# The gated output of a state space layer: four fp32 panels against three fp32r passes with an operand split, and the layer norm behind it cut by column halves

## The reference

```
y = y.transpose(2, 0, 1, 3, 4).reshape(Bsz, S, G * H) + f32(d_skip) * f32(u)
g = jax.nn.gelu(y).astype(u.dtype)
val, gate = jnp.split(g @ w_glu + b_glu, 2, axis=-1)     # w_glu: 1024 x 2048
y = val * jax.nn.sigmoid(gate)
...
x = layer_norm_2(ALPHA * x + (1.0 + g_m) * y, ln_mix_g, ln_mix_b)
u = x * (1.0 + sc_f) + sh_f
y = moe_ffn(u, w_router, w13, w2)          # top 2 of 8 experts, router on u
x = layer_norm_2(ALPHA * x + (1.0 + g_f) * y, ln_ffn_g, ln_ffn_b)
```

## Time and profile before

| | us |
|---|---|
| runs (3) | 2682.57, 2685.78, 2686.11; median 2685.78 |
| profiled execution, its own time | 2683.08 |
| span of its trace | 2681.2 |
| PE busy | 2482.5 (93%) |
| DVE busy | 1778.1 (66%) |
| ACT busy | 1248.6 (47%) |
| first gated product starts | 1731.62 |
| last gated sum done | 1799.11 |
| router sums done | 1824.49 |
| first expert product starts | 1842.56 |

### The profile page before, as it was taken

How to read it: one execution, slowest core, us unless ns; L and a number is a source line. 1 busy time by engine, 2 the same in 40 slices (tenths; PEclk the granted TensorE clock), 3 DMA queues, 4 the chain that set the end, 5 groups by cost and what they waited for, 6 DMA issues and landing times.

```text
span 2681.2 us, 31991 instructions
## 1 busy us (share of the span) xinstructions
PE 2482.5 (93%) x12549; PEld 1974.6 (74%) x12549; DVE 1778.1 (66%) x1920; ACT 1248.6 (47%) x1290; POOL 157.7 (6%) x142
## 2 busy tenths in 40 slices
PE   7999999999999999899799964587999999999996
PEld 6878768878788688799548852236887888888885
DVE  5863457767733488671535559517888888888887
ACT  4432434344323343442224445305676676677674
POOL 0000000000000000000100006400000000000000
PEclk9999999999999999998899986597999999999998
DMA  8757367667671676540235530124998998998994
GB/s 312 270 200 184 84 180 276 247 230 247 247 177 54 207 271 223 178 145 32 94 118 190 195 119 31 63 94 146 347 347 325 349 345 324 348 345 326 346 349 181
DMA packets 303444, 586.15 MB, mean 219 GB/s; under 512 B 61454, under 2 KB 96996, under 8 KB 303212
## 3 DMA queue, kind: packets, MB, share of 16 engines
q1 hardware_dynamic: 285952, 521.07, 56.1%
q0 software_dynamic: 16960, 63.47, 7.2%
q10 hardware_dynamic: 428, 0.15, 0.0%
HBM read 583.59 MB, written 1.06 MB: 218 GB/s over the span
## 4 chain that ended last, share of the span: by engine, by line
PE 85%; DVE 9%; ACT 3%; issue 2%; DMA 0%; POOL 0%; DVEq 0%; SPq 0%; ACTq 0%
PE psum L851 19%; PE psum L853 18%; PE psum L852 18%; PE psum L1315 3%; PE psum L884 3%; PE psum L2518 2%; PE psum L1322 2%; PE psum L1377 2%; PE psum L2015 2%; PE psum L974 2%; DVE ring_r L1051 1%; PE psum L2632 1%; PE psum L1942 1%; PE psum L2655 1%; ACT ring_r L1045 1%
## 5 line engine op out<-in xcount | busy, mean ns | idle before, releaser
L1051 DVE TENSOR_TENSOR ring_r<-ring,ring_r 128x2048 fp32r<-128x2048 f32 x286 | 652.6, 2289 | 302.7 <-ACT ring_r L1045 302.3
L1045 ACT CAST ring_r<-ring 128x2048 fp32r<-128x2048 f32 x286 | 545.3, 1910 | 513.6 <-PE psum L853 424.0
L853 PE MATMUL psum<-ring_r,arena_r 128*128 128x512 f32 (+1 forms) x1560 | 597.3, 383 | 0.0
L851 PE MATMUL psum<-ring_r,arena_r 128*128 128x512 f32 (+1 forms) x1016 | 401.1, 395 | 9.8 <-DVE arena_r L2650 5.2
L852 PE MATMUL psum<-ring_r,arena_r 128*128 128x512 f32 (+1 forms) x1016 | 391.4, 385 | 0.0
L1051 DVE TENSOR_TENSOR ring_r<-ring,tail_r 128x2048 fp32r<-128x2048 f32 x143 | 327.3, 2289 | 96.4 <-ACT tail_r L1045 96.3
L1045 ACT CAST tail_r<-ring 128x2048 fp32r<-128x2048 f32 x143 | 273.1, 1910 | 145.5 <-PE psum L853 140.4
L853 PEld LDWEIGHTS psum<-ring_r,arena_r 128*128 128x128 f32 x1560 | 294.8, 189 | 57.7
L853 PE MATMUL psum<-ring_r,z_r 128*128 128x512 f32 (+1 forms) x840 | 311.1, 370 | 0.0
L851 PEld LDWEIGHTS psum<-ring_r,arena_r 128*128 128x128 f32 x1016 | 192.2, 189 | 57.6 <-issue 18.1
L852 PEld LDWEIGHTS psum<-ring_r,arena_r 128*128 128x128 f32 x1016 | 192.7, 190 | 37.6 <-issue 1.9
(11 more groups left out here) (410 smaller groups left out, 3337.2 us busy)
## 6 DMA issues: line engine op xcount, KB each, us to landing
ring<-in_moe_w SPq DMA_DIRECT2D x264, 1024.0 KB, 6.9
arena<-in_ada_w POOLq DMA_DIRECT2D x48, 1024.0 KB, 9.1
ring<-in_ffn_wg SPq DMA_DIRECT2D x44, 1024.0 KB, 7.3
ring<-in_ffn_wu SPq DMA_DIRECT2D x44, 1024.0 KB, 7.3
ring<-in_ffn_wd SPq DMA_DIRECT2D x44, 1024.0 KB, 6.9
ring<-in_ffn_w SPq DMA_DIRECT2D x33, 1024.0 KB, 5.3
ring<-in_mlstm_w_in SPq DMA_DIRECT2D x8, 2048.0 KB, 8.6
ring<-in_mlstm_w_out SPq DMA_DIRECT2D x4, 2048.0 KB, 7.7
```

Of the source, the lines that this page charges most:

```text
L851: pe.matmul(dst, lhs_low, rhs, start=start, stop=False)
L853: return pe.matmul(dst, lhs, rhs_low, start=False, stop=stop)
L1045: act.copy(upper[i % UPPERS], place(PN[r.key, i])).then_inc(upper_ready, 1)
L1051: dve.tensor_tensor(low, raw, upper[i % UPPERS], ALU.subtract).then_inc(lower_ready, 1)
```

## The change

The gated output is computed in three fp32r passes. The four panels come in the order gate then value, for column half 0 and then 1, each in two halves of k. The first half of panel 0 in high x high w and low x high w stands on PE ahead of `outputs(7)`, the last output sum; its low w follows it. ACT makes the upper parts (`up{i}`) and the upper parts of gelu's result (`xh0`, `xh1`); DVE makes the lower parts. The bias is loaded by SP before the weight panels, split in an upper and a lower part as well, and added in two products of one row. For column half 1 the order is gate t0, value t0, gate t1, value t1. DVE joins the product with the gate row, the residual and the statistics to each quarter (`gated_dve`), so the layer norm of stage 8 starts with the center for tile 0 as soon as that tile's last value sum is there. The router takes tile 0 before tile 1 is transposed.

```diff
-    def ln_dve(dve, step, m, source, ready, between=None, measured=None):
+    def ln_dve(dve, step, m, source, ready, between=None, measured=None, own=None):
...
         def residual(t):
+            if own is not None:
+                own(t)
+                return
...
         def statistics(t):
-            for i in range(2):
-                dve.bn_stats(bn[:, t, i, :], z[:, t, i * 512:(i + 1) * 512]).then_inc(*step.one())
+            if own is None:
+                for i in range(2):
+                    dve.bn_stats(bn[:, t, i, :], z[:, t, i * 512:(i + 1) * 512]).then_inc(*step.one())
...
-                PN["s5", "glu", i] = rg.take()
+                PN["s5", "glu", i] = rg.take(i, over=s5P.after(("gate01", "val01", "gate11", "val11")[i]))
...
+        sp.wait_ge(x_ready, NT * 8)
+        sp.dma_start(z_row[0:1, :], A["s5_b_glu_2"]).then_inc(bias_landed, 16)
         w = rows(A["s5_w_glu_2"][0])
...
-        pool.wait_ge(*s5P.after("y7"))
-        pool.dma_start(z_row[0:1, :], A["s5_b_glu_2"]).then_inc(bias_landed, 16)
...
+        act.copy(glu_ones, ones[0:1, :]).then_inc(*s5A.inc("ones"))
+        act.wait_ge(bias_landed, 16)
+        act.copy(bias_hi, z_row[0:1, :]).then_inc(*s5A.inc("bias"))
         gelu(act, 0)
+        glu_upper_act(act, 0, None)
+        glu_upper_act(act, 1, s5V.after(f"in{S5_UNITS - 1}"))
         gelu(act, 1)
-        for i in range(4):
-            act.wait_ge(*s5P.after(f"glu{i}"))
-            act.activation(sig[:, i, :], bank(2 * i + 1), ACT.Sigmoid).then_inc(*s5A.inc(f"sig{i}"))
+        glu_upper_act(act, 2, s5P.after("y7"))
+        glu_upper_act(act, 3, None)
+        gate_sig(act, 0, 0)
+        gate_sig(act, 0, 1)
+        glu_upper_act(act, 4, s5P.after("gate01"))
+        glu_upper_act(act, 5, None)
+        glu_upper_act(act, 6, s5P.after("val01"))
+        glu_upper_act(act, 7, None)
+        gate_sig(act, 1, 0)
...
+        if half == 0:
+            act.wait_ge(*s5G.after("x13"))
+        act.copy(glu_xh[:, part, :], xT[:, part, :]).then_inc(*s5A.inc(f"xh{half}"))
...
+        low_x(0)
+        glu_lower_dve(dve, 0)
         skip_u(KD - 1)
-        for i in range(4):
-            h_, t = divmod(i, 2)
-            dve.wait_ge(*s5A.after(f"sig{i}"))
-            ins = dve.tensor_tensor(y_sum[:, t, h_ * CHUNK:(h_ + 1) * CHUNK], bank(2 * i), sig[:, i, :], ALU.mult)
+        low_x(1)
+        glu_lower_dve(dve, 1)
+        dve.wait_ge(*s5A.after("bias"))
+        dve.tensor_tensor(bias_low, z_row[0:1, :], bias_hi, ALU.subtract).then_inc(*s5V.inc("bias_low"))
+        for i in range(2, 6):
+            glu_lower_dve(dve, i)
+        dve.wait_ge(lnp_landed, lnp_count(8))
+        for t in range(NT):
+            gated_dve(dve, step, 0, t)
+        for i in range(6, 8):
+            glu_lower_dve(dve, i)
+
+    def gated_dve(dve, step, h_, t):
...
+        dve.wait_ge(*s5A.after(f"sig{h_}{t}"))
+        link(dve.tensor_tensor(gate, gate, lnp[:, 2, cols], ALU.mult))
+        dve.wait_ge(*s5P.after(f"val{h_}{t}"))
+        link(dve.tensor_tensor(total, bank(4 * h_ + 2 * t), gate, ALU.mult))
+        link(dve.scalar_tensor_tensor(total, x[:, t, cols], ALPHA, total, ALU.mult, ALU.add))
+        dve.bn_stats(bn[:, t, h_, :], total).then_inc(*step.one())
...
+        for t in range(NT):
+            pe.wait_ge(*s5A.after("up0"))
+            pe.wait_ge(*s5V.after(f"scan{S5_UNITS - 2 + t}"))
+            value(0, t, 0, False, False, True)
+        pe.wait_ge(*s5V.after("xl0"))
+        for t in range(NT):
+            value(0, t, 0, True, False)
+        outputs(KD - 1)
+        pe.wait_ge(*s5V.after("low0"))
+        for t in range(NT):
+            value(0, t, 0, False, True)
+        pe.wait_ge(*s5A.after("xh1"))
+        for t in range(NT):
+            value(0, t, 1, False, False)
+        pe.wait_ge(*s5V.after("xl1"))
+        for t in range(NT):
+            value(0, t, 1, True, False)
+        pe.wait_ge(*s5V.after("low1"))
+        for t in range(NT):
+            value(0, t, 1, False, True)
+            biased(0, t)
+        for p, tiles in ((1, (0, 1)), (2, (0,)), (3, (0,)), (2, (1,)), (3, (1,))):
+            for t in tiles:
+                for half in range(2):
+                    pe.wait_ge(*s5A.after(f"up{2 * p + half}"))
+                    value(p, t, half, False, False, half == 0)
+                    value(p, t, half, True, False)
+                for half in range(2):
+                    pe.wait_ge(*s5V.after(f"low{2 * p + half}"))
+                    value(p, t, half, False, True)
+                biased(p, t)
...
-    def route_pe(pe):
+    def route_pe(pe, q):
         for t in range(NT):
+            if t > 0:
+                turn_x(pe, q, t)
+            pe.wait_ge(xT_ready, 4 * q + 2 * (t + 1))
...
                         ln_act(act, m, t)
+                        if m == 8 and t == 0:
+                            gate_sig(act, 1, 1)
...
-                    ln_dve(dve, step, m, lambda t: y_sum[:, t, :], [step.now()] * NT)
+                    ln_dve(dve, step, m, None, [s5V.after("low7")] * NT, own=lambda t: gated_dve(dve, step, 1, t))
```

More of the change, by code:

```diff
@@ L380, in s5_dve_order @@
                 names.append(f"y{k - 1}")
-        return names + [f"y{KD - 1}"]
-    s5P = Events(sem("s5_pe"), [f"bt{i}" for i in range(4)] + s5_pe_order() + [f"glu{i}" for i in range(4)])
+        return names + ["xl0", "low0", f"y{KD - 1}", "xl1", "low1", "bias_low"] + [f"low{i}" for i in range(2, 8)]
+    s5P = Events(sem("s5_pe"), [f"bt{i}" for i in range(4)] + s5_pe_order() +
+                 ["gate00", "gate01", "val00", "val01", "gate10", "val10", "gate11", "val11"])
     s5A = Events(sem("s5_act"), ["dt", "mag", "abs", "cos"] + [f"bt{i}" for i in range(4)] + ["phase0", "abs0", "rot0"] +
                  [n for k in range(KD) for n in ((f"phase{k + 1}", f"ct{k}", f"abs{k + 1}", f"rot{k + 1}") if k + 1 < KD
-                                                 else (f"ct{k}",))] + ["gelu0", "gelu1"] + [f"sig{i}" for i in range(4)])
+                                                 else (f"ct{k}",))] + ["ones", "bias", "gelu0", "xh0", "up0", "up1", "gelu1", "xh1", "up2", "up3", "sig00", "sig01"] +
+                 [f"up{i}" for i in range(4, 8)] + ["sig10", "sig11"])
     s5V = Events(sem("s5_dve"), ["lam_dt", "turn", "b_wide"] + s5_dve_order())
@@ L2397, in gelu, with glu_place, glu_high, glu_upper_act @@
         act.wait_ge(*s5V.after(f"y{k1 - 1}"))
-        part = xT[:, k1 - KD // 2:k1, :]
-        act.activation(part, part, ACT.Gelu_apprx_tanh).then_inc(*s5A.inc(f"gelu{half}"))
+        part = slice(k1 - KD // 2, k1)
+        act.activation(xT[:, part, :], xT[:, part, :], ACT.Gelu_apprx_tanh).then_inc(*s5A.inc(f"gelu{half}"))
+        act.wait_ge(*s5A.after(f"gelu{half}"))
+        if half == 0:
+            act.wait_ge(*s5G.after("x13"))
+        act.copy(glu_xh[:, part, :], xT[:, part, :]).then_inc(*s5A.inc(f"xh{half}"))
+    def glu_place(i, of):
+        pn = PN["s5", "glu", i // 2]
+        return of[:, pn.slot, (i % 2) * HALF:(i % 2 + 1) * HALF].rearrange("p (k n) -> p k n", n=CHUNK)
+    def glu_high(i):
+        return glu_hi[2 * (i // 2 % 2) + i % 2]
+    def glu_upper_act(act, i, freed):
+        if freed is not None:
+            act.wait_ge(*freed)
+        act.wait_ge(*landed(PN["s5", "glu", i // 2]))
+        act.copy(glu_high(i), glu_place(i, ring)).then_inc(*s5A.inc(f"up{i}"))
+    def glu_lower_dve(dve, i):
+        dve.wait_ge(*s5A.after(f"up{i}"))
+        dve.tensor_tensor(glu_place(i, ring_r), glu_place(i, ring), glu_high(i), ALU.subtract).then_inc(*s5V.inc(f"low{i}"))
+    def gate_sig(act, h_, t):
+        act.wait_ge(*s5P.after(f"gate{h_}{t}"))
+        act.wait_ge(*s5G.after(f"x{S5_UNITS - 1}"))
+        act.activation(sig[:, 2 * h_ + t, :], bank(4 * h_ + 2 * t + 1), ACT.Sigmoid).then_inc(*s5A.inc(f"sig{h_}{t}"))
     def s5_dve(dve, step):
@@ L2503, in s5_pe, with value @@
                     turn_c(n // 2)
-            if n % 2 == 0 and n >= 4:
+            if n % 2 == 0 and n >= 4 and n // 2 - 2 < KD - 1:
                 outputs(n // 2 - 2)
[L2507 to L2524, removed]
+        def value(p, t, half, x_low, w_low, first=False):
+            of = xT_r if x_low else glu_xh
+            w = glu_place(2 * p + half, ring_r) if w_low else glu_high(2 * p + half)
+            for k in range(KD // 2):
+                pe.matmul(glu_sum(p, t), of[:, KD // 2 * half + k, t * P:(t + 1) * P], w[:, k, :],
+                          start=first and k == 0, stop=False)
@@ new lines, in biased, with glu_sum @@
+        def biased(p, t):
+            h_, is_value = divmod(p, 2)
+            c0 = (1 - is_value) * D + h_ * CHUNK
+            pe.wait_ge(*s5V.after("bias_low"))
+            pe.matmul(glu_sum(p, t), glu_ones, bias_hi[:, c0:c0 + CHUNK], start=False, stop=False)
+            pe.matmul(glu_sum(p, t), glu_ones, bias_low[:, c0:c0 + CHUNK], start=False, stop=True)\
+              .then_inc(*s5P.inc(f"{('gate', 'val')[is_value]}{h_}{t}"))
```

(7 more changed lines are left out.)

20 lines of the change are left out of this document (16 added, 4 removed).

## The result

The changed kernel takes 2650.14 us (median of 4 runs, 2649.16 to 2651.86) for 2685.95 us before (4 runs, 2682.57 to 2688.28): 35.8 us less, a ratio of 0.9868 (95% interval 0.9851 to 0.9885). The forecast was 2653 us, in a range of 2642 to 2662. The profiled execution took 2649.66 us, 33.4 less than that of before.

The account below looks back on a forecast made before the run. The dip before the experts was bound by PE: 6.5 us standing, 67.5 of products, 25.4 of tail. Products ending at 1777.9 plus a 14.6 tail gave 1792.5 for 1824.49, 32.0 less: 2653 us, range 2642 to 2662.

Parts of the forecast that it names:

- Head: Up to panel 0's end: passes ahead of the output sum delay it 0.5 us; panel 0 ends at 1737.6.
- sign for the port: Output sum 7 starting at 1722.7 or later would speak for DVE and POOL excluding each other in SBUF.
- Bias pairs: In each group of the gated output: two one-row passes cost 1.05 us, plus 0.2 for the drain before.
- Price of a pass: Gated output: a 128x512 fp32r product takes 0.228 us at 2.4 GHz, 0.42 at 1.2 GHz.
- Supply: Operands of the groups: `low7` ready at 1757.7, PE at its low parts at 1761.4; margin 3.7 us, no stall.
- Tail: From the products' end to the router's end: 14.6 us for 25.4, table load covered by the router's first half.
- The experts' stage follows: After the router: experts' stage shifts whole, 839 us as now, first load issued at 1771.2.
- dearer head: Rival: SBUF port, panel 0 at 1.2 GHz, or uncovered table load in the tail; 2655 to 2662 us, chance 0.15.
- cheaper pairs: Rival, gated output: bias pairs at 0.46 us give 6.3, passes at 0.215 give 2 more; 2645 us, chance 0.13.
- The transfers: Rival: experts' stream held by its first load, not by PE; gain only 11 us, 2673 us, chance 0.03.
- the clock in the passes: Rival: PE stays at 1.2 GHz, 2687 to 2692 us; half the groups, about 2669; chance 0.02 each.
- passes as dear as fp32: Rival, gated output: three passes no cheaper than an fp32 product; 23.6 us less, 2662 us, chance 0.03.

Follow-up runs that it names:

- e2: Changed kernel with outputs(7) ahead of all passes of the gated output, DVE and ACT left as they are; stage measure 91.93 us for 91.46.
- e3: Changed kernel with one extra root on ACT right behind the last sigmoid, so the root's table loads early; stage measure 90.62 us for 91.46.
- e4: Changed kernel with both tiles transposed and modulated before the router starts; stage measure 94.22 us, fair partner 90.83.
- e6: Kernel before with only the bias load moved to SP ahead of the weight panels; stage measure 118.34 us for 125.91, single time 2681.64 us for 2682.65.
- e9: Kernel before with only the bias load moved to SP, run eleven times; 2677.63 us for 2683.68, ratio 0.9975.
- e7: Changed kernel with the gated output's products fp32 again behind outputs(7) and gelu1, without splits or head start; stage measure 107.52 us for 91.46.
- the combined kernel: Changed kernel with low_x(0) and low0 behind x15, their passes behind outputs(7), low1 ahead of low_x(1), root's table early; 2650.89 us, ratio 0.9879.
- e10: The combined kernel with PE multiplying unused constants in its idle stretches between last gated sum and first expert product; 2642.30 us, ratio 0.9839.
- e5: Changed kernel without the sixteen bias passes of the gated output and PE's wait for bias_low; stage measure 83.38 us, 8.1 less.

## Why the prediction was right, point by point

The likeliest case came in, and the mechanism was the one forecast: cheaper passes, no standing behind gelu, a shorter tail, and an experts' stage that only moves. Some sizes were wrong, and in part they hid each other. From the last scan on, the prediction's sum for the stage was 125.9 - 32.0 = 93.9 us; measured were 91.5. By its own steps, in us:

| step | predicted | measured |
|---|---|---|
| end of `y7`, from the last scan | 9.0 | 10.5 |
| panel 0 ends | 21.0 | 21.4 |
| six groups | 40.3 | 38.0 |
| tail to the router's end | 14.6 | 13.8 |
| router's end to the first expert product | 18.1 | 18.3 |

- **Head.** "I count 0.5 us of delay" was too little: `y7` ends 2.0 later. The output sum starts 2.5 us later: 1.0 is the port (e2), which the prediction had named as its dearer case with 1.2 us or more and not counted, and 1.5 the passes ahead of it, of which eight wait for a `low_x(0)` that takes 3.24 us for 1.22. The sum itself was 0.6 shorter, 3.10 for 3.67. The prediction's own sign for the port, a start at 1722.7 or later, came in with 1724.67. Of the 1.5 us that `y7` is later than forecast only 0.4 is left at the end of panel 0, since the series behind it (8.4 us for the 8.8 forecast) and its end, a bias pair, four passes and a pair (2.5 for 3.2), were shorter than forecast: one error covered the other. And "of which the head gives 6.5 back" counts the standing time alone; by its own numbers panel 0 was to end 12.8 us earlier, and it ended 12.4 earlier. The cover did its part: the passes behind the output sum ran at 1.00 (from 1727.0 on), and the series over ACT and DVE set the end of panel 0 as forecast.
- **Bias pairs.** This is the term that was mis-sized: 1.05 was taken from the fp32 pair, 0.66 is what the two passes take. Over six groups that is 2.3 us, and it is nearly the whole gap of the stage. That the pairs cost far from 1.05 was one of the prediction's own signs of failing; it came, and the time stayed within the range. The reason given, that the cost of changing the number of rows stays, holds, but only for the excess: the fp32 pair took 0.19 more than two plain fp32 instructions (2 x 0.43), the fp32r pair 0.20 more than two plain passes (2 x 0.228). To take the row whole carried the fp32 instructions' own length along; 0.46 + 0.2 would have been the right term. The drain of 0.2 was right (5.69 against 24 x 0.228 = 5.47).
- **Price of a pass**, 0.228 us at 2.4 GHz: right.
- **Supply.** `low7` was done at 1758.0, PE wanted it at 1761.4: no stall, margin as worked out.
- **Tail.** The sum was nearly right, a reason in it was not. The table load was said to be covered by the router's first half by half a microsecond; that half ran in 2.46 us and not in 3.5, at a granted clock of 0.74, since PE came from the passes at 1.00, and so the table load and the root set tile 1, by 0.5 us in this execution and by 0.1 in the second (e3: 0.2 to 0.4 us). A shorter half and an uncovered load in part cancel. The router's split was worth 3.4 us by e4, where the sum had it at 3.5.
- **The bias load.** Before e6 it was priced at its standing time of 4.9 us; alone it is worth 6.0 to 7.6, since the idle time also cost clock (e6, e9).
- **The experts' stage follows.** 839.1 us for 838.6: shifted whole. The first load was issued at 1770.9 for the 1771.2 of the sum.
- **Rivals.** The dearer head came in with the port, the cheaper pairs came in by two thirds (0.66 between 1.05 and 0.46); the first left 0.4 us at the end of panel 0, the second gave 2.3 over the groups. (With the port at 1.2 us the prediction's sum is 2654.2, not the 2654.5 that stands there.) The transfers, the clock in the passes, and passes as dear as fp32 did not come: 1.00 all through the groups, and e7 gives 16.1 us to the passes.

## What to carry to other kernels

A subtraction with two inputs in SBUF is not free cover beside a GpSimd product that is on the path: count whole instructions in turns. Price a stretch of idle PE twice, for its own length and for what runs at half clock after it; here 4.9 us of waiting were worth 6 to 7.6, and useless products in the gaps of a serial tail gave 8 us. When a price is carried from one kind of product to another, carry the excess over the plain product, not the whole. And time a change of several parts part by part: the passes were its main idea, but more than half of the gain lay in an early bias load and in the tail, and the head start gave a microsecond at most.

## What the runs showed of the hardware that was not expected

- Small products feel the clock too: sixteen router instructions of 128x8 took 3.55 us at a granted clock of 0.50 (1.2 GHz, the combined kernel) and 1.95 at 1.00 (2.4 GHz, e10), thirty-two of 128x128 in the gather 6.41 at 0.58 and 3.60 at 1.00.
- In fp32r two one-row passes between 128-row passes take 0.66 us, in fp32 the pair took 1.05, in both about 0.2 more than two 128-row instructions of their kind; left out altogether they gave about 0.94 us a pair (e5).
- The output sum of the same 32 instructions took 3.67 us in the kernel before (clock 0.50) and 3.10 and 2.67 us in two executions of the changed kernel (0.62 and 0.70 over it): the same program, with the clock up earlier in the second.
